# Differential attention projected by head groups: keys, queries and values of heads 0-3, then of heads 4-7, with the attention units placed between the products of the later groups

## What is computed

```
k, v = rmsnorm(x, kv_norm_g) @ kv_w            # k: 8 heads x 2 x 64, v: 8 heads x 128
k    = partial_rope(k)
q    = partial_rope(rmsnorm(x, attn_norm_g) @ w_q)   # 8 heads x 2 x 64
lam  = exp(sum(lv0*lv1)) - exp(sum(lv2*lv3)) + lam_init
for each head h, each block of 128 queries:
    p = masked_softmax(q[h, c] @ k[h, c].T / 8)      # c = 0, 1
    o[h] = (p[0] - lam * p[1]) @ v[h]
o = rmsnorm(o, subln_g) * (1 - lam_init)             # over each head's 128 columns
x = x + o @ w_out
```

## Time and profile before

| | us |
| --- | --- |
| median of 3 runs | 647.74 |
| lowest and highest | 646.26, 647.88 |
| span of the profiled execution | 645.1 |
| TensorE busy in it | 629.7 (98%) |
| VectorE busy | 528.7 (82%) |
| ScalarE busy | 417.3 (65%) |
| GpSimd busy | 36.3 (6%) |

### The profile page before, as it was taken

The page is one execution under the profiler, slowest core; times in us unless marked ns, Lnnn a source line. Parts: engine busy times, 40 slices in busy tenths (PEclk is TensorE's granted clock), DMA queues, the critical chain, the costliest instruction groups (busy, mean ns, idle before and its releaser), DMA issues.

```text
span 645.1 us, 10742 instructions
## 1 busy us (share of the span) xinstructions
PE 629.7 (98%) x3614; PEld 527.9 (82%) x3614; DVE 528.7 (82%) x953; ACT 417.3 (65%) x817; POOL 36.3 (6%) x90
## 2 busy tenths in 40 slices
PE   9999999999999999999999999979999999999995
PEld 8998766678888888888887888768988888888894
DVE  4588688857999888889888646877899898888887
ACT  6554577847766666666677464884866666666666
POOL 1100021200000000000012000150000000000000
PEclk9999999999999999999999999999999999999998
DMA  8677040034455555555525544603455555555521
GB/s 326 250 255 276 2 197 2 1 131 163 164 201 192 196 196 196 196 196 195 173 89 194 197 156 177 250 40 127 168 196 197 196 196 194 189 179 189 189 71 66
DMA packets 21456, 109.11 MB, mean 169 GB/s; under 512 B 2608, under 2 KB 2992, under 8 KB 12464
## 3 DMA queue, kind: packets, MB, share of 16 engines
q1 hardware_dynamic: 21136, 108.48, 47.1%
q10 hardware_dynamic: 288, 0.22, 0.1%
HBM read 107.64 MB, written 1.05 MB: 168 GB/s over the span
## 4 chain that ended last, share of the span: by engine, by line
PE 87%; DVE 8%; ACT 3%; issue 1%; POOL 1%; DVEq 0%; ACTq 0%; POOLq 0%
PE psU L674 21%; PE psA L463 13%; PE psA L464 13%; PE psA L465 13%; PE psU L679 10%; PE psU L900 2%; PE psA L860 1%; PE psU L885 1%; PE psU L474 1%; DVE arena L2107 1%; ACT arena L1500 1%; DVE arena L1818 1%; PE psA L791 1%; PE psU L654 1%; PE psU L653 1%
## 5 line engine op out<-in xcount | busy, mean ns | idle before, releaser
L674 PE MATMUL psU<-hA,win_hi 128*128 128x512 f32 x608 | 190.8, 395 | 0.0
L679 PEld LDWEIGHTS psU<-hA,win_lo 128*128 128x128 f32 x608 | 114.2, 188 | 26.6
L679 PE MATMUL psU<-hA,win_lo 128*128 128x256 f32 x608 | 119.4, 278 | 0.0
L1792 DVE TENSOR_TENSOR win_lo<-stage,win_hi 128x1024 fp32r<-128x1024 f32 x86 | 104.8, 1221 | 0.0
L674 PEld LDWEIGHTS psU<-hA,win_hi 128*128 128x128 f32 x608 | 95.3, 189 | 2.8
L1290 ACT ACTIVATE win_hi<-stage 128x1024 fp32r<-128x1024 f32 x89 | 93.3, 1050 | 5.5 <-PE psA L465 5.5
L1818 DVE SCALAR_TENSOR_TENSOR arena<-arena,prm 128x255 f32<-128x255 f32 (+1 forms) x168 | 77.2, 480 | 3.7 <-ACT arena L1302 0.7
L1700 DVE TENSOR_TENSOR win_lo<-stage,win_hi 128x1024 fp32r<-128x1024 f32 (+3 forms) x50 | 55.8, 1153 | 15.7 <-ACT win_hi L1218 15.5
L463 PE MATMUL psA<-wout_hi,act_hi 128*128 128x512 f32 x168 | 65.9, 392 | 0.3
L464 PE MATMUL psA<-wout_lo,act_hi 128*128 128x512 f32 x168 | 65.6, 390 | 0.0
L465 PE MATMUL psA<-wout_hi,act_lo 128*128 128x512 f32 x168 | 65.4, 389 | 0.0
(11 more groups left out here) (315 smaller groups left out, 1130.8 us busy)
## 6 DMA issues: line engine op xcount, KB each, us to landing
stage<-in_w_ffn_in SPq DMA_DIRECT2D x44, 1024.0 KB, 4.8
stage_out<-in_w_ffn_out SPq DMA_DIRECT2D x44, 516.0 KB, 5.0
stage<-in_w_kv SPq DMA_DIRECT2D x8, 1024.0 KB, 4.9
stage<-in_w_dq SPq DMA_DIRECT2D x4, 1024.0 KB, 4.9
stage<-in_w_dout SPq DMA_DIRECT2D x4, 1024.0 KB, 4.8
stage<-in_w_group SPq DMA_DIRECT2D x3, 1024.0 KB, 4.9
stage<-in_w_nsa_out SPq DMA_DIRECT2D x3, 1024.0 KB, 4.8
stage<-in_w_phi SPq DMA_DIRECT2D x2, 1024.0 KB, 6.0
```

Source lines behind the costliest of these rows:

```text
L674: mm(o, win_hi[:, slot, cs], hA[:, k, :, :].rearrange("p a q -> p (a q)"), start=k == 0, stop=False)
L679: last = mm(o[:, 0:S], win_lo[:, slot, cs], hA_hi[:, k2, :], start=False, stop=k2 == KT - 1)
L1792: last = dve.tensor_tensor(win_lo[:, win, cs], stage[:, slot, cs], win_hi[:, win, cs].bitcast(F32), sub)
```

## The change

The groups are projected in the order keys 0-3, queries 0-3, values 0-3, keys 4-7, queries 4-7, values 4-7 (`DIFF_GROUPS`). `project` has a table `at` of what to do before a k-tile: half the key transposes stand in the second group, half the query transposes and the scores of unit 0 in the third, and units 0 to 3 (all but the last product of unit 3), the other transposes, the scores of unit 4 and `heads_T(0)` in the last three. `PLACE` and `score_banks` give units other banks. After the last group come the rest of units 3 to 7 and the first output chunk, which now stands in two pieces between them (`out_chunk`); `out_first` is gone. VectorE's norm of heads 4-7 is two norms of two heads each; the second halves of the chunks `C_DO + 1` and `C_DO + 2` are GpSimd's, each after a pair of heads.

```diff
+DIFF_GROUPS = ("k", "q", "v", "k", "q", "v")
+PLACE = (0, 1, 1, 0, 0, 1, 0, 1)
...
+        head_banks = [psA[:, 0, :], psT[:, 0], psO[:, 0], psT[:, 1]]
+        def score_banks(u):
+            return psA[:, 0:2, :] if u in (4, 7) else psA[:, 2:4, :] if u == 6 else psU[:, PLACE[u], :, :]
...
-            diff_transpose(0)
-            diff_transpose(1)
-            diff_scores(3)
-            diff_pv(0)
-            for u in range(2, ND):
-                if u + 2 < ND:
-                    diff_scores(u + 2)
-                diff_pv(u - 1)
-                diff_transpose(u)
...
-            heads_T(0)
-            diff_pv(ND - 1)
-            out_project(C_DO, hB_hi, hB_lo, 2 * KVH * TT, 1, 3, next_heads)
+            among = {1: {4: lambda: dk_transposes(0)},
+                     2: {4: lambda: dq_transposes(0), 6: lambda: diff_scores(0)},
+                     3: {0: lambda: diff_scores(1), 2: lambda: diff_transpose(0), 4: lambda: diff_pv(0), 6: lambda: diff_transpose(1)},
+                     4: {0: lambda: diff_pv(1), 3: lambda: diff_scores(2), 4: lambda: dk_transposes(1), 6: lambda: diff_transpose(2), 7: late_q},
+                     5: {3: lambda: heads_T(0), 4: lambda: dq_transposes(1), 6: late_v}}
...
+            def out_chunk(c, t, used):
+                pe_.wait_ge(sem["oT_hi"], 2 * KVH * TT + c + 1)
+                pe_.wait_ge(sem["oT_lo"], 2 * KVH * TT + c + 1)
+                wait_chunk(C_DO + c)
+                if c == 0:
+                    pe_.wait_ge(sem["dprobs"], 4 * (7 if t else 8))
...
+            diff_pv(3)
+            diff_scores(5)
+            diff_scores(6)
+            diff_transpose(4)
+            diff_scores(7)
+            diff_pv(4)
+            out_chunk(0, 1, False)
+            diff_transpose(5)
+            out_chunk(0, 0, True)
+            diff_transpose(6)
+            diff_pv(5)
+            diff_pv(6)
+            heads_T(1)
+            diff_transpose(7)
+            out_chunk(1, 1, False)
+            diff_pv(7)
+            out_chunk(1, 0, True)
+            heads_T(2)
+            for t in range(TT):
+                out_chunk(2, t, t == 1)
+            heads_T(3)
+            out_last(C_DO, hB_hi, hB_lo, 2 * KVH * TT, 1, 3)
...
+            diff_exps(4)
+            split(C_DO + 1)
+            evict(5)
+            out_heads(3)
+            diff_exps(5)
+            diff_exps(6)
+            out_heads(4)
+            diff_exps(7)
             copy_aT(5)
+            head_squares(3)
+            copy_aT(6)
...
-            heads_rstd(dve, 4, 4, "sub1_step", "sub1_rstd")
-            scale_heads(dve, 2, "sub1_scaled")
-            scale_heads(dve, 3, "sub1_scaled")
+            for b in range(2):
+                heads_rstd(dve, 4 + 2 * b, 2, "sub1_step", "sub1_rstd", b)
+                dve.wait_ge(sem["do_ready"], 2 * TT * (b + 3))
+                scale_heads(dve, 2 + b, "sub1_scaled")
```

More of the change, by code:

```diff
@@ new lines, in _ @@
+            for g, kind in enumerate(DIFF_GROUPS):
+                if g >= 2:
+                    pe_.wait_ge(sem["proj_act"], NG + g - 1)
+                    pe_.wait_ge(sem["proj_dve"], NG + g - 1)
+                hh, hl = (hB_hi, hB_lo) if kind == "q" else (hA_hi, hA_lo)
+                project(C_KV + 2 * g, hh, hl, [psA[:, 2 * (g % 2) + t, :] for t in range(TT)], 512, 4,
+                        {0: 2 * KT, 1: 3 * KT}.get(g), at=among.get(g))
+            def out_chunk(c, t, used):
[4 more added lines that the diff above has]
+                    pe_.wait_ge(sem["dprobs"], 4 * (7 if t else 8))
+                for k in range(2):
+                    for n in range(2):
+                        last = out_three(hB_hi, hB_lo, C_DO + c, t, n, k, 2 * c + k)
+                if used:
+                    last.then_inc(sem["in_used"], 1)
@@ new lines, in _ @@
+            out_heads(0)
+            head_squares(0)
+            copy_aT(1)
+            evict(3)
+            out_heads(1)
+            split(C_KV + 9)
+            head_squares(1)
+            diff_exps(2)
+            keys_T(1)
+            split(C_KV + 10)
+            copy_aT(2)
+            out_heads(2)
+            evict(4)
+            split(C_KV + 11)
+            heads_hi(0)
+            diff_exps(3)
+            queries_T(1)
+            split(C_DO)
+            copy_aT(3)
+            head_squares(2)
@@ L1668, in _ @@
+            head_squares(7)
             ffn(1, C_F1, 3)
@@ L2276, in _ @@
+            split(C_KV + 10)
+            diff_maxima(3)
+            turn_rope(4)
+            split(C_KV + 11)
+            heads_lo(0)
             mix_probs(3)
-            maxima(5, 1, "d")
-            copy_aT(3)
+            queries_T(1)
+            split(C_DO)
+            diff_maxima(4)
+            values(5)
             mix_probs(4)
-            maxima(6, 0, "d")
+            split(C_DO + 1, (0,))
+            diff_maxima(5)
+            diff_maxima(6)
+            copy_aT(4)
+            diff_maxima(7)
@@ L2281, in _ @@
             mix_probs(5)
[L2282 removed]
             mix_probs(6)
[L2284 removed]
             mix_probs(7)
+            split(C_DO + 2, (0,))
             copy_aT(7)
[L2287 to L2295 removed]
```

367 lines of the change are left out of this document (170 added, 197 removed).

## The result

The changed kernel takes 659.24 us, the median of 4 runs (656.79 to 661.83), beside 647.81 before: a ratio of 1.018 with a 95% interval from 1.0159 to 1.0201. A second set of 4 runs gave 657.47 (656.86 to 660.21). Beside that set the kernel before took 647.13. The change is 11.4 us slower in the first set and 10.3 in the second; forecast were 656.7 and a range from 652.5 to 660.7.

A forecast was written before the change was run, and what follows sets the result against it. TensorE was taken as the bound, busy 98% of the span. 1.15 + 0.2 + 11.3 - 3.66 = 9.0 us more gave a span of 654.1; with 2.64 us from span to median, 656.7, range 652.5 to 660.7.

The forecast's parts named there:

- The saving: Between the last projected group and the output projection: TensorE's idle 3.66 us is all the new order can save.
- The second group, 1.15 us: Second projected group: TensorE waits 0.27 us for `hB` and 0.88 us for the first rope.
- Weights are no wait here: Second group: no wait for weights, since splits run in the same order and half a group ahead.
- Groups three to six, nothing: Units among the products of groups three to six: no late releaser; breaks between 0 and 1.0 us, 0.2 taken.
- Scores 6, product 4, first piece: 1.75 us: After the last group: TensorE waits 0.1 us for a bank, 0.5 for a copy, 1.15 for exponentials of unit 6.
- The exponentials of unit 7, 2.0 us: Second output piece: these exponentials, held until unit 5's transposes, make TensorE wait 1.92 us and a signal, 2.0 us.
- GpSimd's norm, 2.75 us: Before `heads_T(1)`: TensorE waits 2.75 us for unit 3's squares and then GpSimd's 5.98 us.
- Three waits behind `heads_T`, 4.8 us: Products directly behind `heads_T` wait for split halves: 1.5 us after `heads_T(1)`, 1.65 each after `heads_T(2)` and `heads_T(3)`.
- The clock: TensorE's granted clock in the tail: no cost in the sum; full after the program's last product, longest forecast wait 2.75 us.
- rival 2: TensorE's clock falls to 1.2 GHz behind waits: 659.4 us for one output piece, 662.1 behind two; chance 0.11.
- Rival 4: Faster, 645.4 us: 3.66 us gone, 1.35 paid in the groups, no waits in the tail; chance 0.06.
- within: Time within 1.9 us of no change: waits behind `heads_T` half as long, others gone, 0.8 us; chance 0.04.

The follow-up runs named there:

- e9: e7 with VectorE's lo half of heads 4-5 ahead of its second norm; 657.26 us.
- e4: The changed kernel run again with no edit; 656.86, 657.22, 657.72 and 660.21 us.
- e3: Changed kernel with the transposes of unit 5 ahead of the first output piece instead of behind it; 658.38 us.
- e1: Changed kernel with ScalarE's squares of unit 3 ahead of the exponentials of unit 7 and the copy of unit 5; 659.54 us.
- e5: Changed kernel with squares of unit 3 early and ScalarE's and VectorE's split of heads 2-3 ahead of output chunk 2's weight split; 657.84 us.
- e2: Changed kernel with nine products that nothing reads put into TensorE's 2.53 us wait for GpSimd; 658.31 us.
- e7: Changed kernel with transposes of heads 4-5 ahead of chunk 1's second piece, those of heads 6-7 between chunk 2's pieces; 656.61 us.
- e10: Changed kernel with the key transposes of heads 0-3 one k-tile later in the second group; 658.01 us.
- e11: e8 with the transposes of unit 5 put back behind the first output piece; 646.90 us.
- e8: Changed kernel with all remedies together (transposes moved, squares early, ScalarE's and VectorE's queues reordered); 644.64 us, 0.9952 of the kernel before.
- e12: e8 with the squares of unit 3 put back behind the exponentials of unit 7 and the copy of unit 5; 651.09 us.
- e6: Changed kernel with products that nothing reads put into all six TensorE waits behind the last group; 655.60 us.

## Why the prediction was right, point by point

- **The saving.** 3.66 us of idle time were all that could be won among the products, and it was won. Right.
- **The second group, 1.15 us.** 0.30 for `hB` (0.27 forecast) and 1.55 for the rope (0.88 forecast). The place was right; the size was taken from a rope that ends where it did before, at 356.7, and a TensorE that is there at 355.9. In the new profile the rope ended at 356.72 + 0.43 = 357.15 and TensorE was there at 355.65. "Weights are no wait here" did not hold: ScalarE's split, on which VectorE's queue ahead of the rope depends, waited 1.54 us for its weights' DMA. TensorE's wait for the rope follows that wait from profile to profile: 1.54 and 1.55 us here, 1.35 and 1.36 in e9, 1.19 and 1.18 in the second set of the changed kernel (e4), 1.04 and 1.03 in e3. Where the split has none (e1, e5), TensorE waits 0.47 and 0.50 us, less than forecast.

```profile
352.42 2.01 ACT L1259 ACTIVATE win_hi<-stage 128x1024 fp32r<-128x1024 f32 x2 [1.54 <-DMA stage<-in_w_dq]
```

- **Groups three to six, nothing.** Right: no wait in 62.2 us.
- **Scores 6, product 4, first piece: 1.75 us.** Measured 0.28 + 0 + 1.28 = 1.56 (0.1 + 0.5 + 1.15 forecast). The copy for product 4 was in time.
- **The exponentials of unit 7, 2.0 us.** Measured 2.12, and 2.11 or 2.12 in the profile of every kernel that keeps this order and leaves the wait unfilled (e1, e2, e5, e7, e9, e10, e11). Shown as the cause by e3 and e11.
- **GpSimd's norm, 2.75 us.** Measured 2.53. Here the forecast was right on the wait and incomplete on its worth: I took it as the last thing, and e1 showed ScalarE's split and squares ending together with it. The prediction has no term for that queue. ScalarE's timeline in the changed kernel has it: the split of a weight chunk, squares, and `heads_hi(1)` right behind them at 440.13, while the heads' transposes that it needs were over at 439.25 + 0.66 = 439.91.

```profile
437.65 2.00 ACT L1259 ACTIVATE win_hi<-stage 128x1024 fp32r<-128x1024 f32 x2
...
440.13 0.67 ACT L1673 ACTIVATE hB_hi<-psU,cols 128x512 fp32r<-128x512 f32 x1
```

- **Three waits behind `heads_T`, 4.8 us.** Measured 1.49 + 2.04 + 1.61 = 5.14. The first (1.5 forecast) is for the most part the way through ScalarE and VectorE: e5 has the split out of the way and still waits 1.62, with `heads_hi(1)` 0.5 us behind the transposes. The last (1.65 forecast) was what I said: the lo half came 2.1 us after the transposes began, and e7 took the wait away by cover alone. The second was mis-sized by 0.4: the way would have given some 1.6 again (an estimate from the last one), but VectorE's lo half stood behind its second norm and began at 451.54, 0.46 us after the hi half was there (450.39 + 0.69). What the forecast missed is that cover alone cannot take this one away, since the norm ends there in any case (e7, e9).

```profile
451.54 0.75 DVE L2308 SCALAR_TENSOR_TENSOR hB_lo<-psU,cols,hB_hi 128x512 fp32r<-128x512 f32 x1
```

- **The clock.** This is the step that failed. I put the clock's cost at nothing, and gave rival 2 a chance of 0.11, because the longest wait, 2.75 us, was shorter than an idle stretch with a full clock at the program's end. The clock fell in the first profile after waits of 2.53 and 1.49 us with transposes between them, in e1 after one of 2.11, in e3 after one of 2.03. The one stretch in rows 10 was no bound: shorter waits are followed by a fall in some executions. It cost 1.46 us in the profile (7 slow products, about half of the 2.72 that I had priced for 12). With 0.7 us for the second group, less the 0.2 for breaks that did not show, it makes up the 2.0 us by which the stretch up to `out_last` is longer than forecast (11.0 beside 9.0); the span is only 1.4 us above my 654.1, because the first group happened to begin 0.67 us earlier in this profile, which is luck. The median came 2.5 us above my number. Further falls in the longer executions would account for that (mean granted clock 0.985 and 0.990 beside 0.993), but those executions have no profile, so it is not shown. The Trainium skill's sentence on gaps ("TensorE: Matmul & The Clock Gate", section "Why this matters for your kernels") had the direction right; no single gap of the changed kernel was of the length it warns of, and the clock fell.
- **Rival 4** named its condition: products behind each `heads_T` and the transposes of unit 5 ahead of the first output piece. e8 has both, and is faster, by 3.0 us where I had put 2.3; it has three engines' queues reordered as well, and e7, which has only the products behind the last two `heads_T`, is 9 us slower than the kernel before.
- **The sums.** In the chance for "within" the small waits left over are 0.6 + 2.0 = 2.6 us, not 1.9, which gives 0.1 us in place of 0.8; the chance is not touched by it.

What stays open: where the clock fell in the longer executions, since only one of each set of runs is profiled, and why the weights of the second group landed later in some executions of the new order than in others.

## What to carry to other kernels

When idle time is spread away at one place, walk the engines that prepare the next stage: their queues are what is exposed, and each wait has to be priced with what else ends at the same time. One remedy at a time showed nothing here (e1, e3, e5, e7, e9 and e10 all lay within 2.1 us of 657.5, the median of the changed kernel's eight executions), while all together gained 13 us; put one back into the mended kernel to learn its price. On ScalarE and VectorE, what the next products wait for goes ahead of splits of weights that are needed later.

## What the runs showed of the hardware

TensorE's clock can fall behind a wait of some 2 us, and need not. Waits of 2.11 us (e1, e9, e10), 2.03 (e3), 2.04 (e1, e2, e3) and 2.05 (e10) were followed by 7 or 8 slow products, 0.43 us apart in place of 0.23 (6 behind the one in e10). The same waits of 2.11 and 2.12 us in the changed kernel, e2, e5, e7 and e11, and of 2.04 and 2.02 in the changed kernel and e7, were not. Each of the six waits of 2.98 to 4.66 us behind the last group (e1, e3, e5, e9, e10, e12) was followed by a fall, though in the kernel before the clock was still full 3.6 us after the last product. With the waits filled by idle products the clock was full (e6), and with waits of 1.6 us in all it was full too (e8). Whether such waits add up, or each has its own chance, the runs don't tell.

A small VectorE instruction can take as long as GpSimd's beside it. In e5 VectorE did a 128x4 operation with two inputs from memory in 2.39 us, 0.16 otherwise, from the start to the end of GpSimd's half split:

```profile
439.85 2.39 POOL L1213 TENSOR_TENSOR win_lo<-stage,win_hi 128x1024 fp32r<-128x1024 f32 x1 [7.45 <-DVE win_lo L1767]
439.87 2.39 DVE L324 SCALAR_TENSOR_TENSOR stat<-stat 128x4 f32<-128x4 f32 x1
```

In the changed kernel one took 1.18 us and ended with GpSimd's:

```profile
440.45 2.36 POOL L1213 TENSOR_TENSOR win_lo<-stage,win_hi 128x1024 fp32r<-128x1024 f32 x1 [1.25 <-DVE win_lo L1767]
...
441.65 1.18 DVE L320 TENSOR_TENSOR stat<-stat 128x4 f32<-128x4 f32 x1
```

The Trainium skill ("SBUF — State Buffer", section "SBUF: two separate sides") says that the two engines share a pair of ports as a lock, held for a whole instruction, and that a VectorE operation with two inputs in SBUF needs it where GpSimd's reads SBUF too; the trace agrees, with 2.39 us beside 2.39. I had put no price on GpSimd's new half splits. In e5 this one delayed the first norm by 2.2 us; VectorE went from it into the second norm and the lo half without a pause, so it was part of the queue that chunk 2 waited for.
